# Seven block products for eight in four column blocks of the convolution's input projection

## The reference

```python
h = rms_norm(x, norm_g[l])                        # x: 256 tokens x 4096
proj = jnp.einsum('bsd,dn->bsn', h, w_in[l])      # float32, all projections at once
(aq, ak, av, ai, af, ao, az, bcq, bk, bv, bki, bwi, bz,
 cqkv, cb, ca, cz) = jnp.split(proj, split_points, axis=-1)
...
qkv = jax.nn.silu(causal_depthwise_conv(cqkv, d_conv_w[l]))   # cqkv: 3072 columns, 4 taps
q_c, k_c, v_c = jnp.split(qkv, 3, axis=-1)        # to a gated delta rule, chunks of 64
...
y = jnp.concatenate([y_a, y_b, y_c], axis=-1)     # mLSTM, sparse attention, delta rule
x = x + jnp.einsum('bsm,md->bsd', y, w_out[l])
```

## Time and profile before

| | us |
|---|---|
| median of 3 runs | 1528.72 (1528.32 to 1529.07) |
| the profiled execution, its own time | 1529.63 |
| its span, first to last instruction | 1527.8 |
| TensorE busy | 1523.5 in 6960 matmuls |
| VectorE, ScalarE, POOL busy | 1044.1, 781.0, 362.9 |
| granted TensorE clock, mean | 1.000 |

### The profile page before, as it was taken

How to read it: one execution, slowest core, us unless ns; L and a number is a source line. 1 busy time by engine, 2 the same in 40 slices (tenths; PEclk the granted TensorE clock), 3 DMA queues, 4 the chain that set the end, 5 groups by cost and what they waited for, 6 DMA issues and landing times.

```text
span 1527.8 us, 18922 instructions
## 1 busy us (share of the span) xinstructions
PE 1523.5 (100%) x6960; PEld 1261.3 (83%) x6960; DVE 1044.1 (68%) x1608; ACT 781.0 (51%) x1039; POOL 362.9 (24%) x608
## 2 busy tenths in 40 slices
PE   9999999999999999999999999999999999999999
PEld 7888888888888887888878888888888888888887
DVE  6647555666759865576569677676555877788883
ACT  6745444487544444554545545544445555454543
POOL 9041112230230030126420254344300011110000
PEclk9999999999999999999999999999999999999999
DMA  9886778886788875458765787798876677667667
GB/s 288 286 239 195 224 215 230 217 232 182 227 249 251 252 221 169 147 184 282 246 201 172 228 250 204 236 274 255 231 245 189 191 220 212 190 223 222 210 203 193
DMA packets 207980, 339.35 MB, mean 222 GB/s; under 512 B 53097, under 2 KB 60568, under 8 KB 207632
## 3 DMA queue, kind: packets, MB, share of 16 engines
q1 hardware_dynamic: 184784, 288.66, 62.1%
q0 software_dynamic: 23056, 49.47, 12.4%
q10 hardware_dynamic: 48, 0.02, 0.0%
HBM read 312.81 MB, written 28.73 MB: 224 GB/s over the span
## 4 chain that ended last, share of the span: by engine, by line
PE 98%; DVE 1%; ACT 0%; issue 0%; DMA 0%; DVEq 0%
PE acc L1186 29%; PE acc L1189 29%; PE acc L1188 28%; PE mix L1189 1%; PE mix L1188 1%; PE mix L1186 1%; PE mix L1293 1%; PE mix L1376 1%; PE acc L1202 1%; PE acc L1204 1%; PE acc L1203 1%; PE mix L1204 1%; PE mix L1203 1%; PE mix L1202 1%; PE mix L1365 0%; PE mix L1286 0%
## 5 line engine op out<-in xcount | busy, mean ns | idle before, releaser
L1879 DVE TENSOR_TENSOR w_lo<-w_raw,w_hi 128x1024 fp32r<-128x1024 f32 (+2 forms) x523 | 629.2, 1217 | 356.5 <-ACT w_hi L1517 352.9
L1517 ACT ACTIVATE w_hi<-w_raw 128x1024 fp32r<-128x1024 f32 (+2 forms) x523 | 542.9, 1049 | 436.9 <-PE acc L1189 346.1
L1186 PE MATMUL acc<-w_hi,op_hi 128*128 128x512 f32 (+1 forms) x1868 | 734.2, 393 | 0.3 <-DVE w_lo L1879 0.3
L1189 PE MATMUL acc<-w_hi,op_lo 128*128 128x512 f32 (+1 forms) x1868 | 726.9, 389 | 0.0
L1188 PE MATMUL acc<-w_lo,op_hi 128*128 128x512 f32 (+1 forms) x1868 | 726.7, 389 | 0.0
L1186 PEld LDWEIGHTS acc<-w_hi,op_hi 128*128 128x128 f32 x1868 | 350.8, 188 | 73.9 <-issue 1.3
L1189 PEld LDWEIGHTS acc<-w_hi,op_lo 128*128 128x128 f32 x1868 | 350.6, 188 | 73.5
L1188 PEld LDWEIGHTS acc<-w_lo,op_hi 128*128 128x128 f32 x1868 | 350.9, 188 | 70.8
L888 POOL DMA_DIRECT2D conv_dram<-y x48 | 30.6, 690 | 169.3 <-ACT y L1580 168.5
L888 POOL DMA_DIRECT2D y_dram<-y x32 | 20.6, 716 | 120.2 <-DVE y L2198 68.6
L1049 POOL DMA_DIRECT2D bp_dram<-b_ps x48 | 31.4, 712 | 67.4 <-ACT b_ps L1749 64.0
(11 more groups left out here) (455 smaller groups left out, 1312.4 us busy)
## 6 DMA issues: line engine op xcount, KB each, us to landing
w_raw<-in_w_in_dram SPq DMA_DIRECT2D x367, 512.0 KB, 4.6
w_raw<-in_w_out_dram SPq DMA_DIRECT2D x128, 512.0 KB, 4.5
w_raw<-in_w_in_dram SPq DMA_DIRECT2D x16, 384.0 KB, 3.3
w_raw<-in_a_wuq_dram SPq DMA_DIRECT2D x12, 512.0 KB, 5.7
out_dram<-in_x_dram POOLq DMA_DIRECT2D x7, 512.0 KB, 6.3
conv_dram<-y POOLq DMA_DIRECT2D x48, 64.0 KB, 3.9
y<-conv_dram POOLq DMA_DIRECT2D x48, 64.0 KB, 4.7
w_raw<-in_a_wuqi_dram SPq DMA_DIRECT2D x6, 512.0 KB, 4.7
```

Source lines behind the costliest of these rows:

```text
L1186: nc.tensor.matmul(o, hi[:, kt, tok], hv[:, i, n0:n1], start=(kt == (kts if late else blk["kts"])[0]), stop=False)
L1189: last_mm = nc.tensor.matmul(o, lo[:, kt, tok], hv[:, i, n0:n1], start=False, stop=(kt == blk["kts"][-1]))
L1517: func(split_ap(w_hi, c), w_raw[:, c % RAW_BUFS, 0:n], ACT.Copy).then_inc(hi_ready, 1)
L1879: vec.tensor_tensor(split_ap(w_lo, c), w_raw[:, c % RAW_BUFS, 0:n], split_ap(w_hi, c).bitcast(F32), ALU.subtract).then_inc(lo_ready, 1)
```

## The change

Blocks 2 and 3, and 4 and 5, of the convolution's input become two pairs of kind `cpair` (p = 0 and 1); the output's two pairs are now p = 2 and 3. Each new pair takes channel pairs 0 to 4 with seven products. `CONV_ORDER` gives the order of its chunks: 1 or 2 is a plain chunk of that column block, S a channel pair of both (two chunks). So p = 0 fills chunks 32 to 63, with the second chunk of its seven-product pairs at 37, 43, 49, 53 and 57, and its column blocks end at 58 and 63; p = 1 fills 64 to 95, with 67, 71, 77, 81 and 87, and ends at 88 and 95.

The sums of activations are made in loops 17 to 27: `xs` (VectorE, five steps), `xh` (ScalarE), `xl` (VectorE), for each of five channel pairs. The t tiles of the new pairs lie in parts of `y` and of the region of `cT`. `evs` comes at 57 and 87, and behind it the new `evx`, in which ScalarE scales the sums by `rstd`, twice 128 x 1024. `evn` comes at 58 and 63, 88 and 95: VectorE scales the plain banks and adds, into `conv_stage`, once the taps of the block that used that buffer are done; `evac` of the four blocks is gone.

The tap pieces by the new cursor, old places in brackets: transposes 36, 37; 44, 45; 70, 71 (59, 60); 78, 79 (75, 76); 100, 101 (91, 92); 104, 105 (same). Taps 38, 41; 46, 49; 72, 75 (61, 64); 80, 83 (77, 80); 102, 103 (93, 96); 106, 108 (same). The two of block 1 stay within a loop of where they are now. All that follows, from loop 110 on, keeps its place.

```diff
-SEVEN = [[8, 9, 10, 11, 12], [8, 9, 10, 11, 12, 13, 14]]
+SEVEN = [[0, 1, 2, 3, 4], [0, 1, 2, 3, 4], [8, 9, 10, 11, 12], [8, 9, 10, 11, 12, 13, 14]]
+CONV_SINGLE = 2
+CONV_ORDER = ["1211S1111S1112S22S22S122222", "12S11S1111S11S1222S12222222"]
+X_S = SEVEN[0]
...
-    for j in range(6):
+    for j in range(CONV_SINGLE):
         project("conv", j, C_CQKV + 512 * j)
+    for j in range(CONV_SINGLE, 6):
+        p, q = (j - CONV_SINGLE) // 2, (j - CONV_SINGLE) % 2
+        plain, seven = [i for i in range(KT // 2) if i not in SEVEN[p]], iter(SEVEN[p])
+        of_column = iter(plain)
+        kts = [2 * i + a for token in CONV_ORDER[p] if token in ("S", "12"[q])
+               for i in [next(seven) if token == "S" else next(of_column)] for a in range(2)]
+        block("cpair", j, "h", kts, wide, 512, "w_in", C_CQKV + 512 * j)
...
     for b, x in enumerate(blocks):
-        if x["kind"] != "pair":
+        if x["kind"] == "cpair":
+            p, q = (x["arg"] - CONV_SINGLE) // 2, x["arg"] % 2
+            if q:
+                of_seven = [c for c, (b_, kts) in enumerate(chunks) if b_ == b and kts[0] // 2 in SEVEN[p]]
+                woven[of_seven[0] - 2].append(("four", p))
+                woven[of_seven[-1]] += [("evs", p), ("evx", p)]
+            woven[last[b]].append(("evn", (p, q)))
+        elif x["kind"] != "pair":
             woven[last[b] if b else FIRST_EVAC].append(("evac", b))
...
+    for n, i in enumerate(X_S):
+        for name, more in (("xs", 0), ("xh", 1), ("xl", 2)):
+            woven[NX + 1 + 2 * n + more].append((name, i))
+    at = 0
     for j in range(6):
-        at = weave((end("conv", j) if j else FIRST_EVAC) + (12 if j < 5 else 9), [("cd", 2 * j), ("cd", 2 * j + 1)])
-        at = weave(at, [("conv", 2 * j), ("conv", 2 * j + 1)], 3 if j < 5 else 2)
+        ended = (FIRST_EVAC, end("conv", 1))[j] if j < CONV_SINGLE else end("cpair", j)
+        at = weave(max(at, ended + (12 if j < 5 else 9)), [("cd", 2 * j), ("cd", 2 * j + 1)])
+        at = weave(at, [("conv", 2 * j), ("conv", 2 * j + 1)], (3, 3, 3, 3, 1, 2)[j])
...
+            def evx(p, use):
+                act.wait_ge(rstd_ready, 1)
+                if p == 0:
+                    for use in four_mix(p):
+                        act.wait_ge(emptied[use % 4], use // 4 + 1)
+                else:
+                    for q in range(2):
+                        wait_acc_read(act, p, q)
+                for m in range(M):
+                    func(pair_sum(p)[:, m], pair_sum(p)[:, m], ACT.Copy, scale=rstd[:, m:m + 1]).then_inc(pair_scaled, 1)
...
+            def xs_sums(i, use):
+                raw = x_raw(i)
+                hi, lo = [v[:, 2 * i:2 * i + 2, :].rearrange("p k t -> p (k t)") for v in (op_hi, op_lo)]
+                step(vec.tensor_tensor(raw, hi.bitcast(F32), lo.bitcast(F32), ALU.add))
+                a11, a21, a12, a22 = [raw[:, P * j:P * j + P] for j in range(4)]
+                step(vec.tensor_tensor(a22, a21, a22, ALU.add))
+                step(vec.tensor_tensor(a21, a11, a21, ALU.subtract))
+                step(vec.tensor_tensor(a11, a22, a11, ALU.subtract))
+                vec.tensor_tensor(a12, a12, a11, ALU.subtract).then_inc(s_summed, 1)
...
                 dve.wait_ge(acc_ready, pair_block(p) + 1 + q)
+                if p < 2:
+                    dve.wait_ge(pair_scaled, M * (p + 1))
+                    dve.wait_ge(conv_summed, 2 * (2 * p + q + 1))
                 for m in range(M):
                     k = 2 * q + m
                     dst = pair_sum(p)[:, m, 512 * q:512 * q + 512]
-                    ins = vec.tensor_tensor(dst, plain_banks(p)[k], dst, ALU.add)
-                    if p == 1:
-                        done_bank(ins, four_mix(1)[k])
+                    if p < 2:
+                        ins = vec.scalar_tensor_tensor(conv_stage(CONV_SINGLE + 2 * p + q)[:, m], plain_banks(p)[k],
+                                                       rstd[:, m:m + 1], dst, ALU.mult, ALU.add)
```

More of the change, by code:

```diff
@@ L159, in plan @@
     for b, blk in enumerate(blocks):
-        second = blk["kind"] == "pair" and blk["arg"] % 2
+        second = blk["kind"] in ("pair", "cpair") and blk["arg"] % 2
+        if blk["kind"] == "cpair":
+            if second:
+                p, place = (blk["arg"] - CONV_SINGLE) // 2, [0, 0]
+                for token in CONV_ORDER[p]:
+                    for q in range(2):
+                        if token in ("S", "12"[q]):
+                            b_ = b - 1 + q
+                            chunks.append((b_, blocks[b_]["kts"][2 * place[q]:2 * place[q] + 2]))
+                            place[q] += 1
+                for b_ in (b - 1, b):
+                    last.append(max(c for c, (own, _) in enumerate(chunks) if own == b_))
+            continue
         if second:
@@ L584, in seven_banks @@
         def seven_banks(p):
-            return [bank(use)[:] for use in four_mix(0)] if p == 0 else four_acc()
+            return [bank(use)[:] for use in four_mix(p)] if p % 2 == 0 else four_acc(p)
         def pair_block(p):
-            return next(b for b, x_ in enumerate(blocks) if x_["kind"] == "pair" and x_["arg"] == OUT_SINGLE + 2 * p)
-        def s_hi(i):
+            kind, arg = ("cpair", CONV_SINGLE + 2 * p) if p < 2 else ("pair", OUT_SINGLE + 2 * (p - 2))
+            return next(b for b, x_ in enumerate(blocks) if x_["kind"] == kind and x_["arg"] == arg)
@@ L675, in wait_filled @@
         def wait_filled(eng, use):
-            eng.wait_ge(filled[use % 4], use // 4 + 1)
+            unsignalled = sum(use > use_of["four", p] for p in range(2))
+            eng.wait_ge(filled[use % 4], use // 4 + 1 - unsignalled)
         def wait_emptied(eng, use):
@@ L690, in wait_stored @@
         def wait_stored(eng, kind, arg=0):
+            if kind == "conv" and arg >= CONV_SINGLE:
+                p, q = (arg - CONV_SINGLE) // 2, arg % 2
+                if p == 0:
+                    wait_acc_read(eng, p, q)
+                else:
+                    for use in four_mix(p)[2 * q:2 * q + 2]:
+                        eng.wait_ge(emptied[use % 4], use // 4 + 1)
+                return
             b = next(i for i, x_ in enumerate(blocks) if x_["kind"] == kind and x_["arg"] == arg)
@@ L1239, in seven_second @@
                 pe.wait_ge(t_lo_ready, sevens.index(c) + 1)
[L1240 to L1243, removed]
+                three(c21, *a22, sum_hi[:, 3], sum_lo[:, 3], False, False)
+                three(p5, *s1, sum_hi[:, 0], sum_lo[:, 0], first, end_)
+                three(p6, *s2, sum_hi[:, 2], sum_lo[:, 2], first, end_)
+                three(p7, *s3, sum_hi[:, 1], sum_lo[:, 1], first, end_).then_inc(split_used, 1)
             def gt(_, use):
@@ L1790, in evs @@
                 func(pair_sum(p)[:, 0, 0:512], seven_banks(p)[0], ACT.Copy).then_inc(first_kept, 1)
-            pieces = dict(sh=sh, evs=evs, evac=evac, gt=gt, g2=g2, g4=g4, gb=gb, conv=conv, csq=csq, cn=cn, ce=ce, ca=ca, cv=cv,
+            pieces = dict(xh=xh, evx=evx, sh=sh, evs=evs, evac=evac, gt=gt, g2=g2, g4=g4, gb=gb, conv=conv, csq=csq, cn=cn, ce=ce, ca=ca, cv=cv,
                           ck=ck, cr=cr, co=co, bn=bn, bt=bt, bkn=bkn, bqn=bqn, bkt=bkt, bsc=bsc,
@@ L1884, in seven_sums @@
                 b0, n = c % RAW_BUFS - 1, sevens.index(c)
+                sums = t_parts(c)[0]
                 if n:
```

135 lines of the change are left out of this document (91 added, 44 removed).

## The result

| | before | after | ratio |
|---|---|---|---|
| median of 4 runs each, us | 1528.89 (1528.32 to 1529.62) | 1548.5 (1547.79 to 1551.25) | 1.0131 [1.0114, 1.0149] |
| the profiled execution: own time, span | 1529.6, 1527.8 | 1547.79, 1545.9 | |
| matmuls | 6960 | 6930 | |

A forecast was written before the change was run, and what follows sets the result against it. TensorE was taken to bound the kernel, busy for 1523.5 of 1527.8 us. Span 1527.8 - 6.8 saved + 24.0 of waits + 1 behind loop 110 = 1546.0, at the median's level 1547 us; range 1532 to 1554.

The forecast's parts named there:

- What bounds, and what is saved: TensorE bounds the convolution's stretch; 10 channel pairs by 3 matmuls by 0.2267 us save 6.80 us if TensorE never waits.
- The cover by busy time: Chunks 32 to 57: VectorE's 63 us of work would fit in TensorE's 67.3 us; order decides.
- The lead and the tap piece: A pair's second t_lo has some 0.7 us of lead; a tap piece in the loops before makes TensorE wait.
- the four prices from a full lead: TensorE's wait for one tap piece: 2.7 us four loops before the second chunk, 2.5 three before, 1.7 to 1.9 five before.
- They add up: Once TensorE has waited for a t_lo the lead is gone, so later waits follow whole chains; sum 24.0 us.
- the rival of single waits: The lead comes back between waits in the convolution, only single ones totalling 11.5 us remain: 1534 us, chance 0.18.
- The clock: After waits of 3 us and more TensorE could drop to 1.2 GHz for a chunk or two: 1555 us, chance 0.12.
- half of it kept: Slow work behind six long waits, 2.72 us each, half remaining as loss because the lead grows meanwhile: 8 us.
- Hidden: VectorE and ScalarE fill each other's gaps, waits together stay under 6.8 us: faster, 1522 us with all hidden, chance 0.10.
- late blocks: POOL moves conv blocks 4 and 5 too late, VectorE stands at the transpose: 3 us more, 1550, chance 0.05.
- evs and evx: ScalarE's work behind chunks 57 and 87 delays weight splits: waits of 0.2 us at 61 and at 91.
- The last taps: Taps in loops 102, 103, 106, 108 leave 0.3 us of lead at 110; 0.3 us added, plus 1 behind it.

The follow-up runs named there:

- the last kernel: Changed kernel with the Silu one loop later and a new order of pairs and tap pieces, same ten pairs: 1524.19 us for 1528.97, 0.9972.
- the single pairs: Two kernels: the changed kernel with only one seven-product pair per pair of blocks, at 53 and 77 or at 49 and 87: 1539.59 and 1542.8 us.
- the first kernel with single pairs: Changed kernel with one seven-product pair per pair of blocks, second chunks at 53 and 77: 1539.59 us, one execution (1529.73 for the kernel before).
- two steps of six: Changed kernel with one convolution tap instead of three, leaving out four of a tap piece's six VectorE steps: 1533.79 us, 1.0036 of the kernel before.
- the kernels with the later Silu: Each tap piece's Silu one loop later: in the changed kernel 1536.15 us, with a new order of pairs and tap pieces too 1524.19 us.
- the kernel with another order alone: Changed kernel with other places for pairs and tap pieces, Silu left where it was: 1531.05 us, 1.0011 of the kernel before.
- The other kernel with single pairs: Changed kernel with one seven-product pair per pair of blocks, second chunks at 49 and 87: 1542.8 us, one execution.

## Why the prediction was right

**What bounds, and what is saved.** Right. The pace stays 0.227 us and 30 matmuls are gone. That their 6.80 us are real is seen in the last kernel: 4.8 us faster at the median, 4.6 by span, with 1.4 us of waits left at two places and some of 0.2.

**The cover by busy time.** Right: "By busy time VectorE would still keep up", and "What decides is order". Nearly the same work fits in 168 us when it is ordered otherwise. The sums of activations were put at 2.3 us of VectorE for each pair; measured are 2.5 in step (128-wide steps take 0.33 and not 0.25), and TensorE waits for none of them.

**The lead and the tap piece.** Right: the four prices from a full lead were 2.7, 1.9, 2.5 and 2.7, and measured 2.6, 1.8, 2.45 and 2.6. VectorE waited up to 1.4 us for t_hi in front of a t_lo, as in the earlier trace rows, and ScalarE up to 6.3 for the taps.

**They add up.** Right for the chains, from t_lo to t_lo:

| | 43 to 49 | 49 to 53 | 71 to 77 | 77 to 81 | 81 to 87 |
|---|---|---|---|---|---|
| forecast | 21.3 | 13.7 | 17.9 | 14.3 | 20.8 |
| measured | 21.3 | 13.7 | 17.8 | 14.4 | 21.25 |

So the rival of single waits is out, and the single pairs show it directly.

**The clock.** Here the prediction was right in the total and wrong in its parts. I had given the lower clock a chance of 0.12 and 8 us more; it came in two stretches and cost 5.1 us (2.2 + 2.9). The waits at 53 and 87 were 1.3 and 2.7 instead of 3.5 and 5.1: 4.6 us less. That is in the main one thing, not two errors that happen to cancel. At 49 to 53 VectorE's chain sets the time, 13.7 us whatever TensorE does; a slower TensorE only turns waiting into slow work. My "half of it kept" was wrong for this place: nearly nothing is kept as long as the slow stretch is followed by a wait that is longer than what it lost.
The Trainium skill (TensorE: Matmul & The Clock Gate, "HAM oscillation — how this bites in real kernels") says that a TensorE which has sat idle for long enough starts its next work throttled. The two stretches agree, at 0.50 behind waits of 4.39 and 2.71 us; the first kernel with single pairs, which kept its clock behind 2.72 us, shows that not every such wait does it. The loss added to the forecast's waits would give some 5 us more than the kernel took.

**Where luck helped.** The sum of the forecast's waits is within 0.2 us of the measured one, closer than its terms: 45 and 49, 79 and 81 and the last taps came out 0.25 to 0.3 us shorter each, and the chain from 81 to 87 0.45 longer. That the slow work left the total alone wasn't foreseen either. And 1545.9 is the span of the fastest of four executions; the median, 1548.5, is 1.5 above the forecast.

**Hidden, late blocks.** The order and not the amount kept it from being hidden. Of late blocks there is no sign: from 98 to 330 us, which takes in the transposes of blocks 4 and 5 (302.65 to 320.07), VectorE waits for no conv block, and for no DMA but w_raw, 1.3 us in all.

**evs and evx.** Small and right: 0.4 for 0.2 at 61 and 0.6 for 0.65 at 67. ScalarE's evx in the changed kernel:

```profile
176.15 0.60 ACT L1889 ACTIVATE y<-mix 128x512 f32<-128x512 f32 x1 [1.78 <-PE mix L1286]
179.88 2.20 ACT L1885 ACTIVATE y<-y,rstd 128x1024 f32<-128x1024 f32 x2 [3.13 <-DVE y L2053]
```

The copy takes the 0.60 of the earlier trace rows, the two scalings 2.20 for 2 x 1.06.

**The last taps.** Right in size, loosely reasoned. The prediction calls 0.3 us a lead that is left and adds it as a wait, and puts 1 us more on the squares and norms behind loop 110. Measured is one wait of 1.0 us, at chunk 112, and its cause is the last tap piece itself (ScalarE's Silu, VectorE's w_lo):

```profile
330.53 0.64 ACT L1714 ACTIVATE cT<-cT 128x512 f32<-128x512 f32 x1 [3.00 <-DVE cT L2203]
332.15 2.36 DVE L1978 TENSOR_TENSOR w_lo<-w_raw,w_hi 128x1024 fp32r<-128x1024 f32 x2 [1.65 <-ACT w_hi L1601]
```

The first of the squares comes behind it, at 333.61, and the changed kernel has no later wait that the kernel before has not, but one of 0.2 us. The wait is absent in the kernel before, with two steps of six and in the kernels with the later Silu, and there, at 0.9 to 1.0, in the changed ones that keep the Silu in its place and all six steps. A gap of one loop between the taps of block 4 doesn't remove it: the kernel with another order alone has them in loops 102 and 104, and waits the same 0.96. What their old places, 93 and 96, would be worth was not tried.

## What to carry to other kernels

Where two engines work their queues in order and wait for each other, price a new piece by the chain of waits through it and the lead that is left, not by the busy shares: 72% of an engine's time was here too much in one order and 73% little enough in another. Find the instruction that waits for the other engine ahead of work that is urgent, and put it one loop later; then keep the long pieces away from the places with the shortest lead. A lead once lost wasn't given back here between close places, so the price of each is to be counted from the last wait on, not from rest.

## What the runs showed that was not expected

The clock's fall doesn't follow from the length of a wait alone. Behind 2.71 us at 81 the changed kernel ran 14 matmuls at the lower level; the single pair's kernel had a wait of 2.72 at its chunk 81, with waits of 1.65 and 0.64 ahead of it as the other had 1.89 and 0.65, and went on at its pace. The other kernel with single pairs fell behind a shorter wait, 2.29 us at 49. TensorE in the changed kernel:

```profile
243.28 0.80 PE L1284 MATMUL mix<-tc_hi,op_hi 128*128 128x512 f32 x1 [2.71 <-DVE tc_lo L2000]
243.88 0.63 PE L1285 MATMUL mix<-tc_lo,op_hi 128*128 128x512 f32 x1
244.31 0.63 PE L1286 MATMUL mix<-tc_hi,op_lo 128*128 128x512 f32 x1
```

Behind 2.46 at 87 the clock didn't fall. What decides between these cases stays open.
